# State space mixer: decay sums and sample inputs by broadcast DMA in place of TensorE products

## The chip, the cores and the metric

One Trainium2 chip, one core. The metric is the device time of one execution in microseconds. The engines are TensorE (PE in the rows), VectorE (DVE), ScalarE (ACT), GpSimd (POOL) and SyncE (SP), which only issues transfers here.

## What is computed

Two layers of a decoder over 512 prompt tokens and 8 sample tokens of width 1024: attention and gated linear attention, a squared ReLU layer, a state space mixer, and a second squared ReLU layer. The change lies in the state space mixer alone. Cut to what matters (8 groups of 4 heads, head width 64, state width 128, chunks of 128 tokens):

```python
xdt = x * dt[..., None]                                   # (chunk, token, group, head, 64)
cum = cumsum(dt * a_neg, axis=token)                      # within a chunk
seg = exp(where(causal, cum[t] - cum[s], -inf))
cb = einsum('tk,sk->ts', cm, bm)
y_intra = einsum('ts,jts,sjp->tjp', cb, seg, xdt)
to_end = exp(cum[last] - cum)
u = einsum('sk,sj,sjp->jpk', bm, to_end, xdt)             # into the state of the chunk
state = exp(cum[last]) * state + u
y_inter = einsum('tk,jpk,tj->tjp', cm, state, exp(cum))
```

A sample token is a chunk of length one with a state of its own: state = exp(dt a) state + dt x B, y = state C.

## The kernel before

Everything is in fp32. A fp32 product on TensorE stands in the rows as two MATMUL records (x2 for each product). Weights come in units of 128 x 1024 (512 KB) through a ring of 8 slots, loaded by SyncE as slots come free.

The mixer works group by group (`ssd_mix(g, d, project, products)` on TensorE, `mix(...)` on VectorE and ScalarE, `states(g)` on GpSimd), and each group carries along the six projections of the next one (`project(0)` to `project(5)`: two of x, then B, C, and two of the gate z). Group 0 stands by itself, groups 1 to 6 are three turns of a loop of two groups, and group 7 stands by itself: it has no next group, and products of the output projection (L1095) take the place of the six projections. Each engine runs its instructions in the order in which they are written and waits on semaphores; nearly every VectorE instruction is also waited for before the next (`mdo`, `cdo`).

TensorE's order in a group, with the lines of the profile:
1. `ssd_tokens`: transposes of B (L948) and of the samples (L950); sums of the decays in token order, over a chunk and over samples (L951 to L953); after ScalarE's roots of the group before, the transposes of x (L959).
2. `project(0)` (L517), `sample_outer(g, 0)` (L972): the outer products of the sample inputs with B into PSUM, from `sxdiag`, a diagonal spread that GpSimd makes (L468). Then `ssd_cb` (L979).
3. `project(1)`, `sample_outer(g, 1)`, `ssd_spread` of heads 2 and 3 (L994): a product that spreads the running decay sums of a head over all 128 partitions of a PSUM bank.
4. `project(2)`, `ssd_spread` of heads 0 and 1.
5. `project(3)` with `sample_y` (L1007) between its products, which reads the stepped states and waits for `ssm_stepped`; `ssd_intra` (L1023, L1028), which waits for `seg_ready`.
6. `project(4)`, `ssd_inter` (L1037), `project(5)`, `ssd_norm` (L1044).

ScalarE copies a finished projection into `xe` and `xs` (`conv_in`), makes the tanh of the convolution (`conv_tanh`), and the exponentials: `efeat` (L1384) from the spread sums in PSUM, and `seg` (L1385) from VectorE's differences. At the end of a group it takes the tanh of gate part 1, loads the table of the root (L1399) and takes the roots (L1401, L1403).

VectorE's order in a group: copies of the sums and of the samples (L1959, L1960); sxdt (L1962), xdt (L1967); the normalizing of the group before (L1936, L1938); `step_states(0)` (L1978), adding the outer products from PSUM to the decayed states; `prepare` and the taps of part 0 of the next group (L1882 to L1898); xde (L1993), the masked cb (`cbm`, L1996); `finish` of part 0, taps of part 1; `step_states(1)`; `differences` of heads 2 and 3 (L1983: spread sum less own sum, not above 0, from PSUM to `seg`); finish 1, taps 2; differences of heads 0 and 1; four products seg x cbm (L2013); finish 2, taps 3; the chunk states (L2029 to L2033), and the outputs.

GpSimd loads the states of a group (1 MB), makes `sxdiag`, multiplies the states by their decays in two halves (L477), and stores them.

Of the kernel before, what the change touches and what calls it, by code (L numbers as in the profile page):

```python
# [14 lines left out]
F32 = mybir.dt.float32  # L15
U32 = mybir.dt.uint32
ALU = mybir.AluOpType
# [3 lines left out]
P = 128  # L21
D = 1024
DC = D // P
TP = 512
NB = 8
# [74 lines left out]
PW = 120  # L100
LEAST = -3.0e38
# [40 lines left out]
def build(nc, A):  # L142
    ctx = ExitStack()
    with ctx:
# [118 lines left out]
        dts = sb("dts", [P, 8, NT + 1, CH_ALL], stack=c)  # L263
        dtg = sb("dtg", [P, 2, NT + 1, CJ], stack=c)
        dag = sb("dag", [P, 2, NT + 1, CJ], stack=c)
# [10 lines left out]
        cum = sb("cum", [P, 2, NT, CJ], stack=c)  # L276
        dec = sb("dec", [P, NT, CJ], stack=c)
        toend = sb("toend", [P, NT, CJ], stack=c)
# [13 lines left out]
        ssamp = sb("ssamp", [NB, 3, P], stack=c)  # L292
        sxdt = sb("sxdt", [NB, CJ, CHD], stack=c)
        sadg = sb("sadg", [NB, 2, NB, CJ], stack=c)
        sadec = sb("sadec", [P, NB, CJ], stack=c)

        sxdiag = seg[0:NB].rearrange("k j t q -> k (j t q)").rearrange("k (b c) -> k b c", b=NB)
# [4 lines left out]
        pssm = sb("pssm", [P, CJ, CHD], stack=c)  # L302
        c.close()

# [96 lines left out]
        def _(pool):  # L401
# [59 lines left out]
            def states(g):  # L461

                pool.dma_start(flat(ss0[:]), A["ssm0"][g]).then_inc(sem("ssm_in"), 16)

                if g:
                    pool.wait_ge(sem("y_intra"), g)
                pool.wait_ge(sem("sxdt_ready"), g + 1)
                nc.gpsimd.tensor_tensor(sxdiag, flat(sxdt[:]).unsqueeze(1).to_broadcast((NB, NB, GW)),  # L468
                                        deltac[:].unsqueeze(2).to_broadcast((NB, NB, GW)), ALU.mult).then_inc(
                    sem("sxdiag_ready"), 1)  # L470

                pool.wait_ge(sem("ssm_in"), g * 16 + 16)
                pool.wait_ge(sem("sadec_ready"), g + 1)
                for half in (slice(0, NB // 2), slice(NB // 2, NB)):
                    s = ss0[:, half].rearrange("p b j q -> p (b j) q")
                    decays = sadec[:, half].rearrange("p b j -> p (b j)").unsqueeze(2)
                    nc.gpsimd.tensor_tensor(s, s, decays.to_broadcast((P, NB // 2 * CJ, CHD)), ALU.mult).then_inc(  # L477
                        sem("ssm_decayed"), 1)
# [4 lines left out]
                pool.wait_ge(sem("ssm_out"), g * 16 + 16)  # L483
# [21 lines left out]
        def _(pe):  # L505
# [438 lines left out]
            def ssd_tokens(g, d):  # L944
# [4 lines left out]
                for i in range(3):  # L949
                    pe.transpose(B[7][0:NB, 32 + i * P:32 + (i + 1) * P], conv[:, d, i, TP:T], ident[:])  # L950
                mm(B[7][:, 0:16], tri[:], flat(dag[:, d, 0:NT]), start=True, stop=True)  # L951
                mm(B[7][:, 16:32], ones, flat(dag[:, d, 0:NT]), start=True, stop=True)
                mm(B[7][:, 416:448], ones[0:NB], flat(sadg[:, d]), start=True, stop=True).then_inc(  # L953
                    sem("ssd_turned"), 1)
# [7 lines left out]

            def sample_outer(g, half):

                if half == 0:
                    pe.wait_ge(sem("xdt_ready"), g + 1)
                    pe.wait_ge(sem("sxdiag_ready"), g + 1)
                else:
                    pe.wait_ge(sem("ssm_stepped"), g * 2 + 1)
                for j in range(2):  # L970
                    b = 4 * half + 2 * j
                    x = mm(B[4 + j][:], ssamp[:, 2, :], sxdiag[:, b:b + 2, :].rearrange("k b c -> k (b c)"), start=True, stop=True)  # L972
                x.then_inc(sem("ssm_outer"), 1)
# [9 lines left out]
            def ssd_spread(g, d, heads):  # L983

                for j in heads:
                    if j == 2:
                        pe.wait_ge(sem("cbm_ready"), g + 1)
                    if j == 3:
                        for read in ("small_read", "ssamp_read", "sadec_ready"):
                            pe.wait_ge(sem(read), g + 1)  # L990
                    if j == 0:
                        pe.wait_ge(sem("ssm_stepped"), g * 2 + 2)
                    for t in range(NT):
                        x = mm(B[4 + j][:, t * P:(t + 1) * P], dag[:, d, t, j:j + 1].to_broadcast((P, P)), tri[:],  # L994
                               start=True, stop=True)
                    x.then_inc(sem("decays_spread"), 1)

            def sample_y(g, d, products):


                pe.wait_ge(sem("decays_featured"), g * 4 + 1)
# [11 lines left out]
            def ssd_intra(g):  # L1013

                for j in (2, 3, 0, 1):
                    if j == 2:
                        pe.wait_ge(sem("seg_ready"), g * 4 + 2)
                    if j == 0:
                        pe.wait_ge(sem("seg_ready"), g * 4 + 4)
                        pe.wait_ge(sem("decays_featured"), g * 4 + 4)  # L1020
# [26 lines left out]
            def ssd_mix(g, d, project, products=2 * DC):  # L1047
# [5 lines left out]
                sample_outer(g, 0)  # L1053
                ssd_cb(g, d)
                project(1)
                sample_outer(g, 1)
                ssd_spread(g, d, (2, 3))
                project(2)
                ssd_spread(g, d, (0, 1))
# [17 lines left out]
            for j in range(1, SSD_UNITS):  # L1077
                ssd_project(0, j)
            ssd_mix(0, 0, lambda j, between=None: ssd_project(1, j, between))
# [54 lines left out]
        def _(act):  # L1134
# [195 lines left out]
            run(flat(dts[:, 2]), flat(dts[:, 1]), ACT.Exp).then_inc(sem("dt_expd"), 1)  # L1330
# [917 lines left out]
```

## Time and profile before

| | us |
|---|---|
| median of 3 runs | 1935.43 (1935.29 to 1935.89) |
| the profiled execution's own time | 1935.07 |
| its span, first to last instruction | 1933.3 |
| TensorE busy | 1856.6 |
| VectorE busy | 1065.1 |
| ScalarE busy | 354.3 |
| GpSimd busy | 147.2 |

The mean granted clock of TensorE was 0.96 of full speed (1.00 is 2.4 GHz, 0.50 is 1.2 GHz). Busy time is that of records; on TensorE the records of neighbouring products overlap, so that the chain's lengths are what a product costs. "idle before" in brackets is how long the engine had nothing, and what ended it. "issue" is time in which nothing that the profile shows was waited for.

### The profile page before, as it was taken

Reading aid. Unit: us, or ns where it says so; the run is one execution under the profiler, and the core shown is the slowest. Engines: PE = TensorE matmul, PEld = TensorE weight load, DVE = VectorE, ACT = ScalarE, POOL = GpSimd, SP = SyncE. Lnnn points to the kernel's source line nnn. Section 1 sums busy time; section 2 is a strip of 40 time slices with the busy share of each in tenths; the row PEclk is TensorE's granted clock in tenths of the full one; section 3 lists DMA queues with packets and bytes.
Section 4 is the critical chain, followed back from the end, with each engine's and each line's share of the span. In section 5 each row is a group of like instructions: output and inputs, shape, how many; then the busy total and the mean of one; then the engine's idle time right before and its main releaser. Section 6 shows DMA issues by size and latency. Waiting matters only on the chain.

```text
span 1933.3 us, 23888 instructions
## 1 busy us (share of the span) xinstructions
PE 1856.6 (96%) x8882; PEld 1562.0 (81%) x8882; DVE 1065.1 (55%) x2013; ACT 354.3 (18%) x856; POOL 147.2 (8%) x188
## 2 busy tenths in 40 slices
PE   7999989998999999989999999999999999999995
PEld 5776688776888888878888878888888888888884
DVE  4443753537544454555687778778643544445454
ACT  2322001111220032011222222322110121012100
POOL 0000220000000000000111011101100000000001
PEclk9999959788999999998999999999999999999997
DMA  7111531004545756541123212221303342343221
GB/s 248 58 55 56 174 120 44 24 17 164 223 176 217 267 192 238 195 154 54 49 97 102 91 44 101 95 82 57 112 34 130 110 153 92 146 169 149 88 87 44
DMA packets 47586, 227.43 MB, mean 118 GB/s; under 512 B 7080, under 2 KB 10168, under 8 KB 44416
## 3 DMA queue, kind: packets, MB, share of 16 engines
q1 hardware_dynamic: 37312, 123.74, 18.8%
q0 software_dynamic: 10032, 102.30, 13.8%
q8 instruction: 61, 1.00, 0.2%
q14 instruction: 37, 0.30, 0.1%
q10 hardware_dynamic: 144, 0.09, 0.0%
HBM read 210.78 MB, written 82.40 MB: 152 GB/s over the span
## 4 chain that ended last, share of the span: by engine, by line
PE 87%; DVE 7%; DMA 2%; ACT 2%; issue 2%; POOL 0%; DVEq 0%; SPq 0%; ACTq 0%
PE bank L904 40%; PE bank L517 30%; PE bank L1095 2%; PE bank L994 2%; PE bank L659 1%; PE bank L972 1%; PE bank L1023 1%; PE bank L619 1%; PE bank L603 1%; PE bank L1007 1%; DVE rstd L1435 1%; PE bank L1028 1%; DMA ring<-units 1%; DMA gath<-cache_v 1%; PE bank L1037 1%
## 5 line engine op out<-in xcount | busy, mean ns | idle before, releaser
L517 PE MATMUL bank<-hn,ring 128*128 128x260 f32 x2304 | 553.6, 393 | 5.5 <-DVE hn L1453 4.5
L517 PEld LDWEIGHTS bank<-hn,ring 128*128 128x128 f32 x2304 | 434.1, 194 | 77.0 <-issue 14.3
L904 PE MATMUL bank<-hid,ring 128*128 128x260 f32 x1024 | 231.0, 382 | 0.0
L904 PEld LDWEIGHTS bank<-hid,ring 128*128 128x128 f32 x1024 | 194.6, 190 | 29.9
L904 PE MATMUL bank<-hid,ssum 128*128 128x260 f32 x768 | 174.2, 382 | 0.0
L904 PEld LDWEIGHTS bank<-hid,ssum 128*128 128x128 f32 x768 | 145.9, 190 | 22.4
L904 PE MATMUL bank<-hn,ring 128*128 128x260 f32 x512 | 124.9, 387 | 2.8 <-DVE hnt L1712 2.8
L904 PE MATMUL bank<-hnt,ring 128*128 128x260 f32 x512 | 123.2, 383 | 0.0
L1732 DVE TENSOR_TENSOR u<-bank,p1c 128x260 f32<-128x260 f32 x48 | 20.6, 429 | 184.7 <-PE bank L904 183.1
L904 PE MATMUL bank<-hnt,ssum 128*128 128x260 f32 x512 | 118.9, 385 | 1.8 <-DVE hid L1741 1.8
L904 PEld LDWEIGHTS bank<-hn,ring 128*128 128x128 f32 x512 | 98.3, 192 | 18.6 <-DVE hnt L1712 3.2
L904 PEld LDWEIGHTS bank<-hnt,ssum 128*128 128x128 f32 x512 | 97.9, 191 | 17.5 <-DVE hid L1741 2.2
L904 PEld LDWEIGHTS bank<-hnt,ring 128*128 128x128 f32 x512 | 97.6, 191 | 15.1
L1737 DVE TENSOR_TENSOR u<-bank,u 128x260 f32<-128x260 f32 x48 | 20.6, 429 | 123.0 <-PE bank L904 122.8
L1296 ACT ACTIVATE hid<-hid 128x260 f32<-128x260 f32 x96 | 40.3, 420 | 258.0 <-DVE hid L1738 178.3
L517 PE MATMUL bank<-mixT,ring 128*128 128x260 f32 x224 | 65.7, 459 | 9.9 <-DVE h L1684 9.9
L1898 DVE SCALAR_TENSOR_TENSOR conv<-xe,pg,conv 128x512 f32<-128x512 f32 x96 | 72.2, 752 | 3.4
L1143 ACT ACTIVATE hn<-h 128x520 f32<-128x520 f32 x40 | 25.0, 635 | 262.9 <-DVE h L1768 153.4
L517 PEld LDWEIGHTS bank<-mixT,ring 128*128 128x128 f32 x224 | 50.8, 231 | 25.6 <-DVE h L1684 12.4
L1308 ACT ACTIVATE p1c<-bank 128x260 f32<-128x260 f32 x48 | 18.6, 387 | 244.9 <-PE bank L904 244.9
L904 PE MATMUL bank<-hn,ssum 128*128 128x260 f32 x256 | 61.3, 382 | 0.0
L517 PE MATMUL bank<-yout,ring 128*128 128x260 f32 x256 | 58.1, 391 | 2.4 <-DVE h L1684 2.4
(338 smaller groups left out, 2340.1 us busy)
## 6 DMA issues: line engine op xcount, KB each, us to landing
ring<-units SPq DMA_DIRECT2D x224, 512.0 KB, 4.1
ss<-ssm POOLq DMA_DIRECT2D x8, 1024.0 KB, 5.8
out_ssm<-ss POOLq DMA_DIRECT2D x8, 1024.0 KB, 5.8
out_win_k<-cache_k POOLq DMA_DIRECT2D x8, 1022.0 KB, 8.8
out_win_v<-cache_v POOLq DMA_DIRECT2D x8, 1022.0 KB, 6.4
gath<-cache_k POOLq DMA_DIRECT2D x24, 256.0 KB, 3.8
gath<-cache_v POOLq DMA_DIRECT2D x24, 256.0 KB, 3.7
h<-xT SPq DMA_DIRECT2D x4, 520.0 KB, 5.3
```

The costliest lines, as they stand in the source:

```text
L517: x = mm(half(n), ring[:, s, k], src[:, first + k, cols], start=start and k == blocks[0], stop=last and k == blocks[-1])
L603: mm(B[4 + j][:, 0:(j + 1) * P], qr[rows, j * P:(j + 1) * P], kr[rows, 0:(j + 1) * P], start=True, stop=True).then_inc(sem("scored"), 1)
L619: mm(B[7][AD * e:AD * e + AD, kt * P:TP], vtok[:, kt, AD * e:AD * e + AD], pt[:, PT_AT[kt]:PT_AT[kt] + TP - kt * P], start=kt == 0, stop=k ...
L659: x = mm(out[:, hp, b, :], gath[:, n % SLOTS, i, hp * P:(hp + 1) * P], spt[:, i, b * AH + 2 * hp:b * AH + 2 * hp + 2], start=b == 0 and hp ...
L904: x = mm(bank[:, 0:LO], weight(m, w, q % (DC // 2)), operand(m, q), start=q == 0 and m not in (2, 3), stop=q == every - 1, skip_group_chec ...
L994: x = mm(B[4 + j][:, t * P:(t + 1) * P], dag[:, d, t, j:j + 1].to_broadcast((P, P)), tri[:], start=True, stop=True)
L1095: x = mm(bank(n), ring[:, w, k], yout[:, part * DC + k, cols], start=part == 0 and k == 0, stop=part == 1 and k == DC - 3, skip_group_chec ...
L1143: run(hn[:, k], h[:, k], ACT.Square).then_inc(squares, 1)
L1296: ins = run(out, src, ACT.Relu)
L1732: do(V.tensor_tensor(u2[:], B[5][:, 0:LO], p1c[:], ALU.add), "banks_read")
L1737: do(V.tensor_tensor(u3[:], B[7][:, 0:LO], u2[:], ALU.add), "banks_read")
L1898: cdo(V.scalar_tensor_tensor(out, xe[:, j, tap:tap + TP], pg[:, d, 4 * j + tap:4 * j + tap + 1], out, ALU.mult, ALU.add), "taps_done" if t ...
```

## The change

For all eight groups at once, ahead of group 0, a table is made (`tab`, 100 columns per group): dt, the running sums, the decays of chunks, the decays to the chunk's end, and the sample decays. The running sums of all 32 heads also go as rows to a DRAM scratch (`cums`), from which GpSimd's queue broadcasts four heads per group over all partitions, straight into `seg` in SBUF. The dt-weighted sample inputs of a group go to a second scratch (`sxs`) and come back broadcast (`xb`). The outer products with B become eight `scalar_tensor_tensor` on VectorE, from SBUF. The differences are made in place in `seg`. All of `efeat` is made ahead of the first difference, since it reads what the differences overwrite.

GpSimd, per group:

```diff
-                pool.dma_start(flat(ss0[:]), A["ssm0"][g]).then_inc(sem("ssm_in"), 16)
                 if g:
                     pool.wait_ge(sem("y_intra"), g)
+                else:
+                    pool.wait_ge(sem("tab_begun"), 1)
+                    pool.dma_start(cums, cumrows).then_inc(sem("rows_out"), 16)
+                    pool.wait_ge(sem("rows_out"), 16)
+                pool.dma_start(flat(seg[:]), cums[CJ * g:CJ * g + CJ].rearrange("j t -> (j t)").unsqueeze(0)
+                               .to_broadcast((P, CJ * TP))).then_inc(sem("cums_in"), 16)
+                if g:
+                    pool.wait_ge(sem("ssm_out"), g * 16)
+                pool.dma_start(flat(ss0[:]), A["ssm0"][g]).then_inc(sem("ssm_in"), 16)
                 pool.wait_ge(sem("sxdt_ready"), g + 1)
-                nc.gpsimd.tensor_tensor(sxdiag, flat(sxdt[:]).unsqueeze(1).to_broadcast((NB, NB, GW)),
-                                        deltac[:].unsqueeze(2).to_broadcast((NB, NB, GW)), ALU.mult).then_inc(
-                    sem("sxdiag_ready"), 1)
+                pool.dma_start(sxs[g].rearrange("(b c) -> b c", b=NB), flat(sxdt[:])).then_inc(sem("rows_out"), 16)
+                pool.wait_ge(sem("rows_out"), g * 16 + 32)
+                if g:
+                    pool.wait_ge(sem("ssm_stepped"), g * 2)
+                pool.dma_start(flat(xb[:]), sxs[g].unsqueeze(0).to_broadcast((P, NB * GW))).then_inc(
+                    sem("sx_in"), 16)
                 pool.wait_ge(sem("ssm_in"), g * 16 + 16)
-                pool.wait_ge(sem("sadec_ready"), g + 1)
...
-                pool.wait_ge(sem("ssm_out"), g * 16 + 16)
```

TensorE: the calls of `sample_outer` and `ssd_spread` and both functions are gone; L951 to L953 and one of the three transposes of samples (L950) too. `sample_y` waits for `cbm_ready` in place of an efeat. Ahead of group 0:

```diff
+            pe.wait_ge(sem("dt_folded"), 2)
+            for t in range(NT):
+                x = mm(B[4][0:CH_ALL, t * P:(t + 1) * P], dts[:, 1, t], tri[:], start=True, stop=True)
+            x.then_inc(sem("cums_summed"), 1)
+            mm(B[6][:, 0:NT * CH_ALL], tri[:], flat(dts[:, 1, 0:NT]), start=True, stop=True)
+            mm(B[6][:, NT * CH_ALL:2 * NT * CH_ALL], ones, flat(dts[:, 1, 0:NT]), start=True, stop=True)
+            mm(B[6][:, 2 * NT * CH_ALL:512], ones[0:NB], flat(sad), start=True, stop=True).then_inc(
+                sem("cums_summed"), 1)
+            pe.wait_ge(sem("tab_ready"), 1)
```

ScalarE, in `mix` (and ahead of group 0 a copy of the sums to rows and three exponentials of the table):

```diff
-                act.wait_ge(sem("ssamp_read"), g + 1)
-                run(flat(sadec[:]), B[7][:, 416:448], ACT.Exp).then_inc(sem("sadec_ready"), 1)
                 run(flat(btok[:]), B[6][:], ACT.Copy).then_inc(sem("btok_ready"), 1)
-                act.wait_ge(sem("cum_left"), g + 1)
-                run(flat(dec[:]), flat(cum[:, 1]), ACT.Exp).then_inc(mstep, 1)
-                run(flat(toend[:]), flat(toend[:]), ACT.Exp).then_inc(sem("decay_exps"), 1)
...
+                act.wait_ge(sem("ssamp_read"), g + 1)
+                act.wait_ge(sem("cums_in"), g * 16 + 16)
+                for j in range(CJ):
+                    rows = slice(CHD * (j % 2), CHD * (j % 2) + CHD)
+                    run(efeat[rows, j // 2, :], flat(seg[:, j])[rows, P:TP], ACT.Exp).then_inc(
+                        sem("decays_featured"), 1)
                 for i, j in enumerate((2, 3, 0, 1)):
-                    act.wait_ge(sem("decays_read"), g * 4 + (i + 1))
-                    rows = slice(CHD * (j % 2), CHD * (j % 2) + CHD)
-                    run(efeat[rows, j // 2, :], B[4 + j][rows, P:TP], ACT.Exp).then_inc(sem("decays_featured"), 1)
+                    act.wait_ge(sem("seg_bounded"), g * 4 + (i + 1))
```

The new efeat stand behind the tanh of part 1 of the next group, ahead of this loop. VectorE, in `mix` (a copy of the group's table, `tabg`, takes the place of the copies and differences of the sums, and three copies of `prepare` are gone):

```diff
                 def step_states(half):
-                    dve.wait_ge(sem("ssm_outer"), g * 2 + (half + 1))
+                    if half == 0:
+                        dve.wait_ge(sem("sx_in"), g * 16 + 16)
                     dve.wait_ge(sem("ssm_decayed"), g * 2 + (half + 1))
-                    for j in range(2):
-                        b = 4 * half + 2 * j
-                        s = ss0[:, b:b + 2].rearrange("p b j q -> p (b j q)")
-                        mdo(V.tensor_tensor(s, s, B[4 + j][:], ALU.add), "ssm_stepped" if j else None)
+                    for b in range(4 * half, 4 * half + 4):
+                        s = flat(ss0[:, b])
+                        mdo(V.scalar_tensor_tensor(s, xb[:, b], conv[:, d, 2, TP + b:TP + b + 1], s, ALU.mult,
+                                                   ALU.add), "ssm_stepped" if b % 4 == 3 else None)
...
-                step_states(0)
...
+                def differences(j):
+                    for t in range(NT):
+                        own = F_CUM + CJ * t + j
+                        mdo(V.tensor_scalar(seg[:, j, t], seg[:, j, t], tabg[:, own:own + 1], 0.0, ALU.subtract,
+                                            ALU.min), "seg_bounded" if t == NT - 1 else None)
+
+                dve.wait_ge(sem("decays_featured"), g * 4 + 4)
+                differences(2)
+                differences(3)
+                step_states(0)
                 step_states(1)
-                for i, j in enumerate((2, 3)):
-                    dve.wait_ge(sem("decays_spread"), g * 4 + (i + 1))
-                    differences(j)
+                differences(0)
+                differences(1)
                 if nxt is not None:
                     finish(nxt, 1 - d, 1)
                     taps(nxt, 1 - d, 2)
-                for i, j in enumerate((0, 1)):
-                    dve.wait_ge(sem("decays_spread"), g * 4 + (i + 3))
-                    differences(j)
```

Ahead of group 0 VectorE copies dt and the running sums into the table and takes the sums to the chunk's end; the wait is `tab_ready`, for VectorE and TensorE both.

## Rows read from the trace of the kernel before

**Rows 1.** The page, part 1: busy time, share of the span and instructions.

```profile
PE 1856.6 (96%) x8882; PEld 1562.0 (81%) x8882; DVE 1065.1 (55%) x2013; ACT 354.3 (18%) x856; POOL 147.2 (8%) x188
```

**Rows 2.** The chain in order of time: start, length, engine, line.

```profile
924.00 1.02 PE bank L959 x8
...
1051.58 1.09 PE bank L959 x8
...
1061.59 1.09 PE bank L979 x8
...
1069.70 1.91 PE bank L972 x4
1071.61 1.98 PE bank L994 x16
...
1080.60 1.78 PE bank L994 x16
1082.39 0.44 PE bank L517 x2
...
1092.97 2.50 PE bank L1023 x32
...
1112.80 0.39 ACT gz L1360
...
1377.52 1.09 PE bank L959 x8
```

**Rows 3.** The timeline of TensorE: start, length, line, operation.

```profile
1115.40 1.09 PE L959 MATMUL bank<-ident,conv 128*128 128x128 f32 x8 [0.31 <-ACT ystd L1401]
...
1137.16 2.74 PE L994 MATMUL bank<-tri,dag 128*128 128x128 f32 x16 [1.73 <-DVE cbm L1996]
```

**Rows 4.** The timeline of VectorE.

```profile
1069.06 1.22 DVE L1993 TENSOR_TENSOR turns<-xdt,toend 128x1024 f32<-128x1024 f32 x1
...
1093.85 0.55 DVE L1895 TENSOR_SCALAR conv<-xe,pg 128x512 f32<-128x512 f32 x1 [0.41 <-ACT xs L1345]
1094.43 2.33 DVE L1898 SCALAR_TENSOR_TENSOR conv<-xe,pg,conv 128x512 f32<-128x512 f32 x3
...
1117.51 0.19 DVE L1959 COPY cum<-bank 128x32 f32<-128x32 f32 x1 [3.18 <-issue]
```

**Rows 5.** The timeline of GpSimd.

```profile
1052.88 3.59 POOL L468 TENSOR_TENSOR seg<-sxdt,deltac 8x2048 f32<-8x2048 f32 x1 [13.64 <-DVE sxdt L1962]
1056.45 4.21 POOL L477 TENSOR_TENSOR ss<-ss,sadec 128x1024 f32<-128x1024 f32 x2
```

**Rows 6.** The timeline of ScalarE.

```profile
1077.71 0.48 ACT L1384 ACTIVATE efeat<-bank 64x384 f32<-64x384 f32 x1 [2.36 <-DVE seg L1983]
1078.09 0.62 ACT L1385 ACTIVATE seg<-seg 128x512 f32<-128x512 f32 x1
```

**Rows 7.** Groups by line and shape, 880 to 1540, VectorE: busy, mean ns | idle.

```profile
L1898 DVE SCALAR_TENSOR_TENSOR conv<-xe,pg,conv 128x512 f32<-128x512 f32 x96 | 72.2, 752 | 3.4
L1983 DVE TENSOR_SCALAR seg<-bank,cum 128x128 f32<-128x128 f32 x128 | 44.9, 351 | 9.3 <-PE bank L994 3.6
L2013 DVE TENSOR_TENSOR seg<-seg,cbm 128x512 f32<-128x512 f32 x32 | 22.1, 692 | 1.1
...
L2031 DVE TENSOR_TENSOR std<-st,dec 128x256 f32<-128x256 f32 x24 | 10.2, 425 | 0.8
...
L1988 DVE TENSOR_SCALAR yT<-conv,pg 128x520 f32<-128x520 f32 x16 | 7.9, 491 | 0.6
```

**Rows 8.** TensorE in slices: length, busy (records), granted clock, DMA share, GB/s.

```profile
1138.00:1140.00 2.00, 2.00 (x12) 0.59 0.00 0
1140.00:1142.00 2.00, 2.00 (x6) 0.56 0.00 0
```

**Rows 9.** The page, part 6: DMA issues, KB each, median us to landing.

```profile
ss<-ssm POOLq DMA_DIRECT2D x8, 1024.0 KB, 5.8
...
out_pssm<-pssm POOLq DMA_DIRECT2D x8, 128.0 KB, 1.9
```

More of the change, by code:

```diff
@@ L100 @@
 PW = 120
+F_DT, F_CUM, F_DEC, F_END, F_SAMPLE = (CJ * i for i in (0, NT + 1, 2 * NT + 1, 3 * NT + 1, 4 * NT + 1))
+TAB = F_SAMPLE + CJ * NB
 LEAST = -3.0e38
@@ L948, in ssd_tokens @@
                     pe.transpose(B[6][:, t * P:(t + 1) * P], conv[:, d, 2, t * P:(t + 1) * P], ident[:])
[L949 to L954, printed above, removed]
+                for i in range(2):
+                    x = pe.transpose(B[7][0:NB, i * P:(i + 1) * P], conv[:, d, i, TP:T], ident[:])
+                x.then_inc(sem("ssd_turned"), 1)
                 for t in range(NT):
@@ L981, in ssd_cb @@
                 x.then_inc(sem("cb_ready"), 1)
[L983 to L996, printed above, removed]
             def sample_y(g, d, products):
-                pe.wait_ge(sem("decays_featured"), g * 4 + 1)
+                pe.wait_ge(sem("cbm_ready"), g + 1)
                 pe.wait_ge(sem("ssm_stepped"), g * 2 + 2)
@@ L1413, in _ @@
             gate(0, 0, 1)
+            act.wait_ge(sem("cums_summed"), 1)
+            run(cumrows, B[4][0:CH_ALL, :], ACT.Copy).then_inc(sem("tab_begun"), 1)
+            act.wait_ge(sem("cums_summed"), 2)
+            by_chunk = lambda first, count: B[6][:, first:first + count * CH_ALL].rearrange(
+                "p (t g j) -> p g t j", t=count, g=CG)
+            by_group = lambda first, count: tab[:, :, first:first + count * CJ].rearrange(
+                "p g (t j) -> p g t j", j=CJ)
+            run(by_group(F_DEC, NT), by_chunk(NT * CH_ALL, NT), ACT.Exp).then_inc(sem("tab_begun"), 1)
+            run(by_group(F_SAMPLE, NB), by_chunk(2 * NT * CH_ALL, NB), ACT.Exp).then_inc(sem("tab_begun"), 1)
+            act.wait_ge(sem("dt_folded"), 3)
+            run(by_group(F_END, NT), by_group(F_END, NT), ACT.Exp).then_inc(sem("tab_ready"), 1)
             mix(0, 0, 1)
@@ L1967, in mix @@
                     mdo(V.tensor_tensor(xdt[:, 2 * i:2 * i + 2], pair(4 + i),
-                                        dtg[:, d, 2 * i:2 * i + 2].unsqueeze(3).to_broadcast((P, 2, CJ, CHD)),
+                                        steps[:, 2 * i:2 * i + 2].unsqueeze(3).to_broadcast((P, 2, CJ, CHD)),
                                         ALU.mult), "xdt_ready" if i else None)
@@ L2030, in mix @@
                         continue
-                    mdo(V.tensor_tensor(std1[:], st[:, t - 1], dec[:, t].unsqueeze(2).to_broadcast((P, CJ, CHD)),
+                    mdo(V.tensor_tensor(std1[:], st[:, t - 1], decays[:, t].unsqueeze(2).to_broadcast((P, CJ, CHD)),
                                         ALU.mult))
@@ L2072, in _ @@
             gate(0, 0, 1)
+            by_group = lambda first, count: tab[:, :, first:first + count * CJ].rearrange(
+                "p g (t j) -> p g t j", j=CJ)
+            do(V.tensor_copy(by_group(F_DT, NT + 1), dts[:, 0].rearrange("p t (g j) -> p g t j", g=CG)))
+            dve.wait_ge(sem("tab_begun"), 3)
+            sums = lambda i: B[6][:, i * NT * CH_ALL:(i + 1) * NT * CH_ALL].rearrange(
+                "p (t g j) -> p g t j", t=NT, g=CG)
+            do(V.tensor_copy(by_group(F_CUM, NT), sums(0)))
+            do(V.tensor_tensor(by_group(F_END, NT), sums(1), by_group(F_CUM, NT), ALU.subtract), "dt_folded")
+            dve.wait_ge(sem("tab_ready"), 1)
             mix(0, 0, 1, None)
```

82 lines of the change are left out of this document (32 added, 50 removed).

## The prediction

> **What bounds the kernel now.** I read the page first, then the chain that ended last, then the timelines of single groups. On the page TensorE is busy for 96% of the span and VectorE for 55% [rows 1]; what matters is the stage of the eight groups, the only one that changes. The chain in order of time runs there through TensorE almost alone [rows 2]: the transposes of x of group 0 begin at 924.00, those of group 7 at 1377.52, so seven groups take 453.5 us. In the group that begins at 1051.58 the reader should see one product after another, with no pause in which a unit of weights waits. Only at the end of a group does the chain leave TensorE: projection 5 ends at 1112.80, ScalarE then gates, loads its table and takes roots, and the next transposes begin at 1115.40, after TensorE sat idle for 0.31 [rows 2, 3]. These 2.60 us are ScalarE's, and work taken from TensorE inside them brings nothing. Two groups are longer: VectorE begins them 3.18 us late, at the turn of its loop, and TensorE waits 1.73 us for its mask product [rows 3, 4].
>
> **A yardstick.** I call the start of the x transposes p0; an undisturbed group lasts 1115.40 - 1051.58 = 63.82. I walk through a changed group by the order of the code and the durations of the rows, and ask when the next p0 comes.
>
> **What leaves TensorE.** The outer products of the samples (L972) come twice per group, 1.91 each time (one stands), the spread decay sums (L994) take 1.98 and 1.78 [rows 2]: together 7.58 us per group. The small products L951 to L953 and one transpose (0.8 us) lie in the 2.60 us of ScalarE, so they are worth nothing except in group 0. Were TensorE alone the bound, eight groups would save 61 us.
>
> **What VectorE must now deliver.** TensorE starts projection 3, with the sample outputs between its products, only once all states are stepped. Before, it got there at 1082.39, that is p0 + 30.81 [rows 2]. Without the 7.58 it is there at p0 + 23.2: transposes 1.09, cb 1.09, and projections 0 to 2 at 7.01 each (L994 ends at 1071.61 + 1.98 = 1073.59, the next begins at 1080.60). When has VectorE stepped the states?
> - Taps of part 1 read what ScalarE copies out of projection 1. That ends at p0 + 16.2; from the end of a projection to the first tap 0.88 us pass (projection 3 ends at 1092.97, the tap on its copy begins at 1093.85) [rows 2, 4]. So p0 + 17.1. VectorE is there at about the same time: before, xde began at 1069.06 [rows 4], p0 + 17.5; without the first states (1.4 and a wait of 0.5) and three little copies of 0.3 each, and with xde, cbm and one finish (1.2 + 0.7 + 0.7) behind it, that is p0 + 17.3. GpSimd's decays end earlier now, since its 3.59 us of sample products are gone [rows 5], and VectorE's normalizing beside them is less disturbed, which gives VectorE perhaps 1 us back. I take 17.1.
> - The four taps take 0.58 + 2.36 = 2.94 [rows 4]: p0 + 20.0.
> - New wait. VectorE may not overwrite the sums before ScalarE has made all four efeat, and ScalarE makes them behind the tanh of part 1, which needs these taps. One efeat takes 0.48 and the next instruction starts 0.38 after it; the tanh and the exponential of 512 take about 0.6 [rows 6]. 0.55 + 3 x 0.4 + 0.55 = 2.3: p0 + 22.3. VectorE idles here, in every group, where it had none before.
> - Differences of heads 2 and 3. From PSUM 128 columns take 351 ns. A column costs 1.04 ns (256 more of them 692 - 425 = 267), so 218 of the 351 are fixed. From SBUF a tensor_scalar of 520 columns takes 491 in all, less than its columns alone would at that rate (542) [rows 7], so it goes at twice the rate and 128 columns should take 491 - 392 x 0.52 = 287. With 30 ns between them 8 take 2.54: p0 + 24.8.
> - The states. Eight scalar_tensor_tensor of 256 columns, all from SBUF, in place of four additions. 512 columns take 752; 256 fewer are worth 267 [rows 7]. 485 + 30 each, 4.1 in all: p0 + 29.0, where the transfers have landed.
>
> So TensorE, ready at 23.2, waits until 29.0: **5.8 us of the 7.58 come back as a wait.** Behind it the chain is as before: from 1082.39 to 1115.40, 33.01 us. VectorE has slack there (its differences of heads 0 and 1, a finish, a tap and four products end near p0 + 38.5, the projection near 39.6). The group lasts 29.0 + 33.0 = 62.0, 1.8 less than now.
>
> **The clock.** After the wait of 1.73 us the granted clock fell: the slices of 2 us behind it read 0.59 and 0.56, so about 3.4 us at 1.2 GHz in place of 2.4 [rows 8], and lost 1.7 us. A wait of 5.8 us is longer, and it comes in seven groups. I charge 1.7 us for each, and bound it from 0 (if the fall lay within the wait) to 3.4 (twice as long). The Trainium skill, "TensorE: Matmul & The Clock Gate", Part 1, says that idle time throttles the array to half and that the cost is half of the throttled time, and it shows a kernel that is throttled anew at each wait; the trace agrees in its one-wait case, and it is what speaks against this change.
>
> **The other kinds of group.** Group 0 has no earlier group to normalize, but its taps of part 1 hang on projection 1 as well, so it lasts the same. In the two groups at the loop's turn VectorE starts 2.4 later, of which 1.0 is covered by that projection: 1.4 more each. Group 7 has no next group: no taps, so the efeat are early, and VectorE has stepped by about p0 + 18 while TensorE arrives at 23.2. There the full 7.58 is gained. Sum of groups 0 to 6: 7 x (62.0 + 1.7) + 2 x 1.4 = 448.8 against 453.5, **4.7 less**.
>
> **The preparation.** Ahead of group 0, TensorE makes seven products (16 passes; 12 of 128 columns at 1.98/16 = 0.12 and 2 of 256 at twice that, 2.0 us), ScalarE two exponentials (0.35 and 0.4), VectorE a copy and a difference from PSUM (0.35 each), ScalarE one more (0.35): 4.0 us with the hand-overs, all serial behind the last projection, 0.8 given back by the small products gone from group 0: +3.2, and half a clock loss, 0.8 (this idle time is near 1.9 us). Between 2.5 and 6; I take 4.0. VectorE's other new work there (the tables' copy, the sample sums) lies beside projections.
>
> **DMA.** Per group two broadcasts of 1 MB and a row of 8 KB come to GpSimd's queue. Nearest rows: 1 MB of states lands in 5.8 us, 128 KB in 1.9 [rows 9]. The sums are sent at the end of the group before, some 33 us ahead of their use, and push the load of the states back by about 5 us, to about p0. The samples: row written by p0 + 2.4, broadcast landed by p0 + 8.3, decays (4.21 before [rows 5]) done by p0 + 7, all wanted at p0 + 24.8. Below, this costs nothing; above, it decides from 22 us for the samples' broadcast. I take nothing. In group 0 all four transfers follow each other, and the samples land near p0 + 15, still early.
>
> **Sum.** The profiled execution took 1935.07 (median of the runs 1935.43). 1935.07 - 4.7 - 7.6 + 4.0 = 1926.8; put to the median, **1927**.
>
> **Where a rule and a row part.** The nearest row of the same instruction is the 351 ns from PSUM. By it the eight differences would take 0.5 us more per group, and the sum would be 1931. The Trainium skill, "VectorE: DVE Perf Modes", section on mode 2x_2P, has tensor_scalar in fp32 from SBUF at two columns a cycle and gives no such mode to an instruction with two tensors, as the states' step now is. The 491 ns decide for 287.
>
> **Rivals.**
> - *The clock stays low for longer* (slower). At 3.4 us lost per wait: 7 x 1.7 = 11.9 more, **1939**, slower than now. The sign turns at 2.8 per wait. For it: the wait is three times as long as the one seen. Against: the fall also begins inside it, where it costs nothing. 0.19.
> - *No clock loss*: **1915**. Against it [rows 8]; for it, that the fall may end inside the wait. 0.09.
> - *VectorE is hidden, TensorE is the bound*: 61 less the 4 of the preparation: **1878**. It needs states stepped 5.8 us earlier than walked, and the taps hang on projection 1. 0.04.
> - *Broadcasts from one row are slow*: at 30 us in place of 5.8, 7 us per group late: **1980**. No row shows a broadcast. 0.05.
> - Forecast: 0.63.
>
> The range takes in the clock's price down to about 0 and up to 3.4 and half a microsecond per group in the walk: 1912 to 1942. What this kernel's measurement can tell from no change is about 0.2%, 3.9 us. Below 1931.5 lie most of the forecast and the two fast rivals: 0.59; within 0.2% the rest of the forecast and part of the first rival: 0.20; above it 0.21.
>
> **What would show it.** L972 and L994 gone; a wait of about 5.8 us of TensorE ahead of projection 3, ended by VectorE's step of the states, in groups 0 to 6 and not in 7; VectorE idle some 2.3 us for efeat; differences at 287 ns, steps at 485; granted clock of 0.5 for 3 to 4 us behind each wait; groups of 63.7. Wrong it would be if TensorE waited less than 4 us there or more than 7, if the releaser were a DMA, or if the low clock lasted past 5 us.

## The result and the profile after

The changed kernel took 1986.3 us (median of 4 runs, 1977.7 to 1999.5) against 1935.7 before: a ratio of 1.0263, 95% interval 1.0231 to 1.0295, slower by about 51 us. I had said 1927, with 1942 as the end of the range. The direction and the size are both wrong.

The profiled execution took 1987.23, its span 1985.4. The start of the x transposes, p0, divides the stage. Before, the groups 0 to 6 took 63.8 each, and 67.3 and 67.2 at the loop's turns. Now they take 76.1, 67.1, 67.6, 71.0, 74.8, 77.9 and 75.2: 509.7 in all against 453.6, so 56.1 more. From p0 of group 7 to the wait ahead of L1118 (now L1112) it is 62.95 against 70.74, so 7.8 less. p0 of group 0 comes at 927.45 in place of 923.92, 3.5 later. The sum is 51.8 of the 52.1 us by which the span grew; what lies outside this stage changed by 0.3. On the page, the line that answers to [rows 1] shows TensorE busy for only 4 us less, though products of some 61 us are gone: those that are left must have taken longer.

```profile
PE 1852.4 (93%) x8520; PEld 1567.1 (79%) x8520; DVE 1056.6 (53%) x2017; ACT 352.6 (18%) x836; POOL 128.7 (6%) x205
```

Group 2 on TensorE, the timeline: start, length, line, in brackets the idle time ahead and what ended it.

```profile
1070.65 1.09 PE L974 MATMUL bank<-ident,conv 128*128 128x128 f32 x8 [1.11 <-ACT ystd L1393]
1071.58 7.18 PE L535 MATMUL bank<-hn,ring 128*128 128x260 f32 x32
1078.60 1.05 PE L982 MATMUL bank<-conv 128*128 128x128 f32 x8
1079.49 14.19 PE L535 MATMUL bank<-hn,ring 128*128 128x260 f32 x64
1100.03 1.24 PE L535 MATMUL bank<-hn,ring 128*128 128x260 f32 x2 [6.35 <-DVE ss L1980]
1101.05 0.42 PE L995 MATMUL bank<-conv,ss 128*128 128x1 f32 x2
...
1115.76 2.57 PE L1011 MATMUL bank<-seg,xdt 128*64 128x128 f32 x32
```

This answers to [rows 2, 3]. L972 and L994 are gone, and in their place stands one wait of 6.35 us, ended by VectorE's last step of the states (29.4 us after p0). The 1.11 us ahead of L974 were 0.31 before; the small products are gone from a stretch that ScalarE bounds, and this is worth nothing, as said. What the reader should see next is the length of projection 3: from 1100.03 to 1115.76 it takes 15.7 us, where it took 10.6 [rows 2].

VectorE in the same group (timeline), then the two new kinds by shape (880 to 1540: busy, mean ns | idle), then ScalarE's four efeat.

```profile
1088.12 2.33 DVE L1898 SCALAR_TENSOR_TENSOR conv<-xe,pg,conv 128x512 f32<-128x512 f32 x3
1093.26 2.55 DVE L2000 TENSOR_SCALAR seg<-seg,tabg 128x128 f32<-128x128 f32 x8 [2.81 <-ACT efeat L1373]
1095.84 4.13 DVE L1980 SCALAR_TENSOR_TENSOR ss<-xb,conv,ss 128x256 f32<-128x256 f32 x8
```

```profile
L2000 DVE TENSOR_SCALAR seg<-seg,tabg 128x128 f32<-128x128 f32 x128 | 36.6, 286 | 23.8 <-ACT efeat L1373 19.5
...
L1980 DVE SCALAR_TENSOR_TENSOR ss<-xb,conv,ss 128x256 f32<-128x256 f32 x64 | 31.0, 485 | 2.8
```

```profile
1091.02 2.14 ACT L1373 ACTIVATE efeat<-seg 64x384 f32<-64x384 f32 x4
```

The walk holds step by step: 286 and 485 ns where 287 and 485 were worked out from [rows 7], and the new wait for efeat. The transfers are hidden. The two broadcasts land in 4.8 and 5.0 us, where the load of the states took 5.8 before; that load, behind a broadcast now, takes 7.5. GpSimd's timeline of group 2 and the page's DMA issues:

```profile
1071.19 0.51 POOL L484 DMA_DIRECT2D sxs<-sxdt  x1 [12.43 <-DVE sxdt L1964]
1073.49 0.53 POOL L488 DMA_DIRECT2D xb<-sxs  x1 [1.79 <-DMA sxs<-sxdt]
1074.04 3.77 POOL L496 TENSOR_TENSOR ss<-ss,tab 128x1024 f32<-128x1024 f32 x2
```

```profile
seg<-cums POOLq DMA_DIRECT2D x8, 1024.0 KB, 4.8
ss<-ssm POOLq DMA_DIRECT2D x8, 1024.0 KB, 7.5
xb<-sxs POOLq DMA_DIRECT2D x8, 1024.0 KB, 5.0
```

The samples' broadcast lands near 1078.5, 17 us before its first use. The granted clock of TensorE in group 2 (slices of 2 us: length, busy, granted clock, DMA share, GB/s):

```profile
1094.00:1096.00 2.00, 0.00 (x0) 1.00 0.59 174
1096.00:1098.00 2.00, 0.00 (x0) 0.63 0.23 88
...
1100.00:1102.00 2.00, 1.97 (x6) 0.50 0.00 0
...
1108.00:1110.00 2.00, 2.00 (x6) 0.50 0.03 8
1110.00:1112.00 2.00, 2.00 (x13) 0.95 0.00 0
```

The clock falls inside the wait and stays at 1.2 GHz for 10 us after it, through two thirds of projection 3. In group 4 the clock returns only at 1264, 25 us after the wait, behind projection 3 and the products of seg:

```profile
1238.00:1240.00 2.00, 1.35 (x5) 0.50 0.00 0
...
1260.00:1262.00 2.00, 2.00 (x18) 0.50 1.06 393
1262.00:1264.00 2.00, 2.00 (x18) 0.55 0.85 217
1264.00:1266.00 2.00, 2.00 (x11) 1.00 0.43 176
```

From such slices the time at 1.2 GHz can be added up: a slice of 2 us that reads c holds 4 x (1 - c) us of it, of which I count TensorE's busy share. At the low clock while working, the groups 0 to 6 spend 26, 9, 10, 11, 25, 26 and 26 us behind their waits, and group 7, which has no wait there, none. Group 4 is 74.8 us long; with 62.65 for a group without any fall (measured below) that is 12.1 more, half of its 25.

### The profile page after: what moved, and what is told of

The parts are those of the page before. It is cut to its first block, busy times and chain, and to the rows that moved or that the text cites. A ratio compares the mean times of both kernels' runs of the same rounds, so it can differ in the third digit from the quotient of the medians.

```text
span 1985.4 us, 23102 instructions
## 1 busy us (share of the span) xinstructions
PE 1852.4 (93%) x8520; PEld 1567.1 (79%) x8520; DVE 1056.6 (53%) x2017; ACT 352.6 (18%) x836; POOL 128.7 (6%) x205
## 4 chain that ended last, share of the span: by engine, by line
PE 81%; DVE 11%; issue 3%; ACT 2%; DMA 2%; DVEq 0%; POOL 0%; ACTq 0%; SPq 0%
PE bank L922 39%; PE bank L535 27%; PE bank L1089 2%; PE bank L677 2%; PE bank L1011 1%; DVE conv L1898 1%; PE bank L995 1%; DVE ss L1980 1%; DVE yrstd L1936 1%; PE bank L637 1%; PE bank L621 1%; PE bank L1016 1%; DVE rstd L1438 1%; DVE seg L2000 1%; DMA ring<-units 1%
## 5 line engine op out<-in xcount | busy, mean ns | idle before, releaser
L535 PE MATMUL bank<-hn,ring 128*128 128x260 f32 x2304 | 600.6, 415 | 55.6 <-DVE ss L1980 43.7
L535 PEld LDWEIGHTS bank<-hn,ring 128*128 128x128 f32 x2304 | 455.3, 205 | 129.8 <-DVE ss L1980 46.1
L922 PEld LDWEIGHTS bank<-hid,ssum 128*128 128x128 f32 x768 | 146.0, 190 | 22.3
L922 PE MATMUL bank<-hn,ring 128*128 128x260 f32 x512 | 124.8, 386 | 2.9 <-DVE hnt L1715 2.9
L922 PEld LDWEIGHTS bank<-hn,ring 128*128 128x128 f32 x512 | 98.3, 192 | 18.6 <-DVE hnt L1715 3.3
L995 PEld LDWEIGHTS bank<-conv,ss 128*128 128x128 f32 x256 | 71.9, 290 | 18.1
L922 PE MATMUL bank<-hn,ssum 128*128 128x260 f32 x256 | 61.3, 382 | 0.0
```

The lines of the kernel that those rows point to most:

```text
L535: x = mm(half(n), ring[:, s, k], src[:, first + k, cols], start=start and k == blocks[0], stop=last and k == blocks[-1])
L922: x = mm(bank[:, 0:LO], weight(m, w, q % (DC // 2)), operand(m, q), start=q == 0 and m not in (2, 3), stop=q == every - 1, skip_group_chec ...
L995: x = mm(B[6][:, n:n + 1], flat(ss0[:, b, 2 * i:2 * i + 2, :]), conv[:, d, 3, TP + b:TP + b + 1], start=True, stop=True, skip_group_check= ...
```

## The experiments

Theory A: all of the loss is TensorE's wait ahead of projection 3 and a low clock that outlives it. Rivals: the transfers or VectorE's new work slow TensorE by themselves (B). Within theory A, the clock stays low because of what TensorE works on when it comes back (A1), or because the wait is long (A2). The ratio is against runs of the kernel before on the same chip (its medians 1935.7 to 1936.6). The fourth column has the length of a group in which the clock never fell and which is no turn of the loop.

| kernel | us, median | ratio (95%) | group, undisturbed | low clock at work per group |
|---|---|---|---|---|
| changed | 1986.3 | 1.026 (1.023 to 1.030) | none | 9 to 26 |
| e1 states first | 1907.5 | 0.984 (0.980 to 0.988) | 57.6 | 0; 13 and 21 at the turns |
| e2 products apart | 1962.4 | 1.015 (1.012 to 1.018) | none | 12 to 13 |
| e3 fill | 1953.0 | 1.008 (1.005 to 1.010) | 62.65 | 0; 24 and 21 at the turns |
| e4 before, with a wait | 2052.2 | 1.060 (1.054 to 1.066) | none | 11 to 26 |
| e5 steps before taps | 1878.6 | 0.970 (0.968 to 0.972) | 56.0 | 0 |
| e6 efeat early | 1972.9 | 1.018 (1.016 to 1.020) | none | 3 to 25 |
| e7 states first, unrolled | 1882.8 | 0.972 (0.969 to 0.974) | 57.5 | 0 |
| e8 before, products apart | 1949.0 | 1.006 (1.004 to 1.007) | none | 3 to 13 |
| e9 e5, unrolled | 1872.8 | 0.967 (0.964 to 0.971) | 56.0 | 0 |
| e10 one product | 1912.8 | 0.988 (0.985 to 0.992) | none | 4 to 5 |

The last column leaves out the short fall of 1 to 3.4 us behind the preparation that some show in group 0.

**e4, the wait alone, in the kernel before.**

```diff
+                pe.wait_ge(sem("seg_ready"), g * 4 + 1)
                 project(3, sample_y(g, d, products))
```

> The kernel before, with one more wait on TensorE ahead of projection 3, for the first product of seg and cbm of the same group, which comes 5.8 us later than TensorE does. No broadcast, no new VectorE work. Theory A: the same fall of the clock and the same slow return, so about 5.8 + 9 us per group in seven groups and somewhat less in group 7: 2025 to 2050 us. Rival B (the slow return in the changed kernel comes of its broadcasts or its steps of the states): the clock returns after about 3.4 us as it did behind the wait of 1.7 us in the kernel before, so 5.8 + 1.7 per group: about 1990 us.

It took 2052, even above the range of theory A. The wait is 5.8 to 6.2 us in groups 0 to 6, nearly as long as in the changed kernel. Here is the timeline of TensorE and slices behind it, of group 1:

```profile
1040.77 1.23 PE L517 MATMUL bank<-hn,ring 128*128 128x260 f32 x2 [6.20 <-DVE seg L2014]
```

```profile
1042.00:1044.00 2.00, 2.00 (x9) 0.50 0.00 0
...
1062.00:1064.00 2.00, 2.00 (x16) 0.50 1.05 393
1064.00:1066.00 2.00, 2.00 (x22) 0.82 0.85 231
```

The fall is the same, and the return comes 24 us after the wait, as in the changed kernel's longer cases, without a broadcast and without a new VectorE instruction. The groups of 81 to 82 us are 63.8 + 5.8 + 12; groups 3 and 5 took 78 and 80. Rival B is out as the cause of the slow return.

**e3, work in place of the wait, in the changed kernel** (FILL is 14; nobody reads these products).

```diff
+                pe.wait_ge(sem("xdt_ready"), g + 1)
+                for k in range(FILL):
+                    mm(B[5][:, 0:LO], ones, hn[:, k % DC, 0:LO], start=True, stop=True)
                 project(3, sample_y(g, d, products))
```

> The changed kernel with 14 products of 260 columns (about 6.1 us) put ahead of projection 3 on TensorE, whose results nobody reads, so that it works through most of the time in which it waited. VectorE's and GpSimd's work and every transfer are the same. Theory A (the loss is the fall of the clock behind an idle array): the granted clock stays at 1.00 in groups 0 to 6 except perhaps at the loop's turn, projection 3 takes 10.6 us again, a group about 62.6, in all 1918 to 1930 us; group 7, which had no wait, is 6 us longer. Rival B (transfers or VectorE slow TensorE): projection 3 still takes 13 to 20 us, in all above 1975.

Groups 1, 2, 4 and 6 now take 62.65 to 62.8, with the clock at 1.00 throughout. They answer to the 62.0 of my walk, and to the changed kernel's own groups of 67 to 78 us, under the same transfers and the same VectorE work. The whole is 1953, not 1918 to 1930, because at the loop's turns a rest of the wait was left, and I had not given a rest of 3 us its price; without the excess of these two groups, 27 us, it would be 1926. Group 7, which had no wait to fill, is 6.1 us longer, as expected. TensorE and the slices in group 3:

```profile
1155.31 0.71 PE L536 MATMUL bank<-hn,ring 128*128 128x260 f32 x2 [2.90 <-DVE ss L1984]
```

```profile
1154.00:1156.00 2.00, 0.69 (x5) 1.00 0.00 0
1156.00:1158.00 2.00, 2.00 (x9) 0.50 0.00 0
...
1178.00:1180.00 2.00, 2.00 (x18) 0.52 0.90 248
1180.00:1182.00 2.00, 2.00 (x11) 1.00 0.36 145
```

2.9 us idle cost 24 us at the low clock; group 3 took 76.9. A2 is weakened here: this wait is shorter than half of the others and the fall lasts as long as the longest.

**e2, what follows the wait.**

```diff
-                project(3, sample_y(g, d, products))
+                outputs = sample_y(g, d, products)
+                project(3)
+                for m in range(products - 1):
+                    outputs(m)
```

> The changed kernel with projection 3 made in one piece and the 16 products of the sample outputs (128 x 1) in one block behind it, not between its products; TensorE's wait stays where it is. Theory A1 (the clock stays low behind the wait because projection 3 is mixed with one-column products): the clock is back within about 5 us of the end of the wait, before projection 3 is over, and of the 9 us that the clock costs per group some 6 or 7 come back: 1935 to 1950 us. Rival A2 (the length of the wait alone sets how long the clock stays low, 10 to 25 us): nothing changes beyond 1%, 1975 to 2000 us.

It took 1962, between the two, and the trace says why. TensorE in group 1, timeline and slices:

```profile
1025.40 9.93 PE L535 MATMUL bank<-hn,ring 128*128 128x260 f32 x32 [6.46 <-DVE ss L1983]
1035.16 4.59 PE L995 MATMUL bank<-conv,ss 128*128 128x1 f32 x32
1039.67 4.71 PE L1011 MATMUL bank<-seg,xdt 128*64 128x128 f32 x32
```

```profile
1028.00:1030.00 2.00, 2.00 (x6) 0.50 0.00 0
1030.00:1032.00 2.00, 2.00 (x9) 0.80 0.00 0
1032.00:1034.00 2.00, 2.00 (x11) 1.00 0.00 0
...
1038.00:1040.00 2.00, 2.00 (x11) 0.50 0.13 51
```

With plain products behind the same wait of 6.4 us the clock is back at about 1030.8, 5.4 us on. Then it falls a second time, at about 1037.6, in a stretch in which TensorE was never idle: during the block of 16 one-column products. All seven groups show both: the clock is back 5.3 to 6.1 us after the wait, waits of 9 us at the turns included, and falls again in the block. So A1 holds for the first fall, A2 does not, and the block pays for a fall of its own.

**e10, the price of the wait when nearly all one-column products are gone.** 15 of 16 products of the sample outputs are left out per group, so the samples' y is not computed.

```diff
                     for n in range(m * 2 * NB // (products - 1), (m + 1) * 2 * NB // (products - 1)):
+                        if n < 2 * NB - 1:
+                            continue
```

> The changed kernel with 15 of the 16 one-column products of the sample outputs left out in each group (the last one stays and signals), so that the samples' y is not computed; the wait of 6.4 us ahead of projection 3 and all else stays. It prices the return of the clock behind this wait when plain products follow. If the one-column products hold the clock low: 5 to 7 us at the low clock while TensorE works, some 3 us lost, groups of about 62.6 - 3.4 + 3 = 62, in all about 1915 us. If the length of the wait does it: 9 to 25 us of low clock as in the changed kernel, groups of 64 to 74, about 1960 us.

It took 1912.8, as A1 had it, with waits of 6.35 us as before. TensorE in group 2, timeline and slices:

```profile
1080.75 8.87 PE L535 MATMUL bank<-hn,ring 128*128 128x260 f32 x30 [6.35 <-DVE ss L1982]
```

```profile
1082.00:1084.00 2.00, 2.00 (x6) 0.50 0.00 0
1084.00:1086.00 2.00, 2.00 (x9) 0.78 0.00 0
1086.00:1088.00 2.00, 2.00 (x11) 1.00 0.00 0
```

The clock is back 3.8 to 4.7 us after each of the seven waits, TensorE works 4 to 5 us at the low clock, and the groups take 61.3. So behind plain products the low clock costs what I had charged or a little more, about 2.2 us. It is the one-column products between those of projection 3 that make 4.5 to 13 of it.

**e8, the block alone, in the kernel before** (the edit of e2, no wait added).

> The kernel before (no wait ahead of projection 3) with projection 3 in one piece and the 16 one-column products of the sample outputs in one block of about 4.6 us behind it. If a dense row of one-column products alone lets the clock fall, though TensorE is never idle, the granted clock reads 0.5 behind it in every group, for 3 to 10 us, and the kernel is slower by 1.0 (the block itself) plus 2 to 5 us per group: 1955 to 1985 us. If only idle time lets it fall, the clock stays at 1.00 and the kernel takes 1936 to 1945 us.

It took 1949, between the two expectations, as the low clock was short: 3.4 us in most groups. But it came in every group, in six of the eight without any wait of TensorE longer than 0.3 us. TensorE's timeline in group 1, where the block is followed by products of seg at the low clock:

```profile
1027.07 3.98 PE L1007 MATMUL bank<-conv,ss 128*128 128x1 f32 x32
1030.97 4.71 PE L1023 MATMUL bank<-seg,xdt 128*64 128x128 f32 x32
```

In groups 3 and 5, where a wait of 2 us stands ahead of L994, the low clock at work comes to 12 or 13 us, 6 behind the wait and 7 behind the block. Idle time is not needed for the clock to fall.

**e6, a shorter wait.** The four efeat move to the start of ScalarE's work on the group (behind btok).

> The changed kernel with the four efeat moved to the start of ScalarE's work on a group; nothing else. VectorE's idle time of 2.8 us ahead of the differences goes and TensorE's wait ahead of projection 3 shrinks from 6.4 to about 3.5 us. Theory A with a cost in proportion to the wait: the low clock shrinks too, from 9.6 to about 5 us lost per group, so the groups take 65 and the whole about 1935 us. Theory A with a slow return that hardly depends on the wait (once the clock is low, projection 3 with its one-column products holds it there): 2.8 us per group come back and little more, 1960 to 1975 us.

It took 1972.9, inside the second expectation. The wait is 3.6 us in place of 6.35 (6.3 in place of 9.1 at the turns), and the low clock at work is 24, 24, 3, 25, 10, 25 and 24 us. It is not in proportion to the wait. Groups 2, 4 and 6 have the same wait to a hundredth and the same products behind it, but the clock is back 4, 11 and 25 us after the wait, and they take 61.6, 64.9 and 71.4 us. The timeline of groups 2 and 6:

```profile
1102.48 1.10 PE L535 MATMUL bank<-hn,ring 128*128 128x260 f32 x2 [3.56 <-DVE ss L1980]
...
1378.21 0.71 PE L535 MATMUL bank<-hn,ring 128*128 128x260 f32 x2 [3.56 <-DVE ss L1980]
```

The same holds for repeated runs of the changed kernel: 1978 to 2000 us, where the kernel before, with far less low clock, stayed between 1929 and 1942 in all sets of runs. I can't say from the rows what decides how long it is.

**e1, the states first.** The theory's use: bring VectorE's answer forward.

```diff
+                step_states(0)
+                step_states(1)
                 dve.wait_ge(sem("decays_featured"), g * 4 + 4)
                 differences(2)
                 differences(3)
-                step_states(0)
-                step_states(1)
```

> The changed kernel with the step of the states moved ahead of the differences of heads 2 and 3, right behind the taps of part 1 (nothing else is changed). Theory A (the wait of TensorE ahead of projection 3 and the low clock behind it are the whole loss): VectorE ends the taps about 19.8 us after the start of the x transposes, the steps about 24.0, TensorE is there at 23.0, so the wait shrinks from 6.4 to about 1 us and the clock mostly stays up; a group takes about 57 us where it took 67 to 78, the two at the loop's turn some 60 to 65. In all about 1885 to 1900 us. Rival B (the new steps or the broadcasts slow something besides the wait, such as TensorE's reads): the groups stay above 62 us, in all over 1925.

It took 1907.5. The wait is 1.0 us in the groups within the loop's turns, and the clock stays up; they take 57.6, where 57 was expected. At the turns the wait is 3.8 and the low clock 13 and 21 us, so these two groups take 66.4 and 70.1, more than the 60 to 65 I gave them, and the whole is above my 1885 to 1900.

**e7, e1 with the loop of groups 1 to 6 written out.**

> e1_states_first with the loop of groups 1 to 6 written out on TensorE, ScalarE and VectorE (same instructions and waits, constants in place of registers). If VectorE's late start of 3.2 us at the loop's turn is the jump back, it goes: no wait of 3.8 us in groups 3 and 5, no fall of the clock there, all groups 57.6, in all about 1885 us. If it is the fetch of more code than is held, it stays or comes more often, up to every group: 1905 to 1960 us.

It took 1882.8, with all six groups at 57.5 to 57.8. VectorE's first copy of group 3, which had come 3.2 us late at the turn [rows 4], now follows at once (no idle time in brackets):

```profile
1098.80 0.42 DVE L1927 SCALAR_TENSOR_TENSOR gz<-gz,bank 128x260 f32<-128x260 f32 x1
1099.23 0.21 DVE L1957 COPY tabg<-tab 128x100 f32<-128x100 f32 x1
```

**e5, the states before the taps, efeat early, the products of seg before taps 2, the sample taps last.** Same instructions, same loop.

```diff
+                step_states(0)
+                step_states(1)
                 if nxt is not None:
                     finish(nxt, 1 - d, 0)
                     taps(nxt, 1 - d, 1)
...
                 dve.wait_ge(sem("decays_featured"), g * 4 + 4)
-                differences(2)
-                differences(3)
-                step_states(0)
-                step_states(1)
-                differences(0)
-                differences(1)
+                for j in (2, 3, 0, 1):
+                    differences(j)
...
-                    sample_taps(nxt, 1 - d)
```

> The changed kernel in another order, the same instructions: ScalarE makes the four efeat at the start of the group; VectorE steps the states behind cbm, ahead of finish 0 and the taps of part 1, then all differences, all products of seg and cbm, finish 1, the samples' outputs, taps 2 and 3, the chunk states, and only then the sample taps. By the walk VectorE has stepped the states at about 19.9 us after the start of the x transposes (22.3 at the loop's turn), ahead of TensorE's 23.0 in every group, and the products of seg stand when TensorE wants them. Theory A: no wait above 1.1 us, no fall of the clock in groups 1 to 6, groups of 56.5 to 57.5 us (up to 62 at the turn), in all 1872 to 1888 us. Rival: another wait takes its place (seg, chunk states) and brings the low clock again: above 1900 us.

It took 1878.6, within what theory A said. VectorE steps the states from 18.2 to 22.3 us after p0 (1042.05), ahead of TensorE:

```profile
1060.22 4.13 DVE L1980 SCALAR_TENSOR_TENSOR ss<-xb,conv,ss 128x256 f32<-128x256 f32 x8
```

TensorE doesn't wait for it. What is left are waits of 0.5 to 1.4 us ahead of the norm product, behind which the clock did not fall:

```profile
1040.04 1.14 PE L1032 MATMUL bank<-turns,normc 128*128 128x260 f32 x4 [0.63 <-DVE turns L2059]
```

**e9, e5 written out.**

> e5_steps_before_taps with the loop of groups 1 to 6 written out on TensorE, ScalarE and VectorE. The waits of 1.4 us ahead of the norm product in groups 2, 3 and 5, which follow VectorE's late start at the turns, should go: groups 1 to 6 all 56.0, 5.5 us less than e5_steps_before_taps, about 1873 us. If writing out costs instruction fetches elsewhere, no gain or a loss: 1878 to 1890.

It took 1872.8, 63.8 us or 3.3% below the kernel before. Groups 1 to 6 all take 56.04 us, 7.8 less than 63.8: the 7.58 us of removed products, and 0.2 that I have not placed.

## Why the prediction was wrong

1. **What leaves TensorE, 7.58 us per group.** Right: e9's groups are 7.8 shorter, and group 7, which has no wait, lost 7.8 in the changed kernel itself.
2. **The walk on VectorE.** Right in each term but one: taps end at 19.8 (20.0), differences 2.55 (2.54), states 4.13 (4.1), the end at 29.3 (29.0). The four efeat follow each other every 0.54 us, not 0.4, so their wait was 2.81 for 2.3. The wait of TensorE was 6.35 for 5.8, and a group with the clock held up takes 62.65 for 62.0. Over seven groups this is 4.5 us. At the turns the wait was 9.1, that is 2.7 longer where I had 1.4.
3. **The price of the clock.** This is the term that failed. I charged 1.7 us per wait, from one wait of 1.73 us [rows 8], with 3.4 as the upper bound, 7 x 1.7 = 12 in all. The groups lost 509.7 - 7 x 62.65 - 2 x 2.7 (the longer waits at the turns) = 66 us, 9.4 per group, from 4.5 to about 13. In the profiled executions the miss is 1987.2 - 1926.8 = 60.4: 54 of the clock (66 - 12), 4.5 and 2.6 of point 2, and less than 1 the other way from the rest. That the low clock would last past 5 us I had named as a sign of being wrong; it lasted 9 to 26 us of work. The row from which I priced was that of a wait ahead of L994 and a plain projection. The wait of the changed kernel stands ahead of projection 3, between whose products stand one-column products. Behind plain products the same long wait costs about 2.2 us (e10); behind these, 4.5 to 13 (changed kernel), and once as little as 1.7 (e6, group 2, behind 3.6 us). I had bounded the cost by the length of the fall that I had seen, and not asked what TensorE would be doing while it came back. My slower rival had the place and the sign, but 3.4 as its price.
4. **What the low clock costs.** By the Trainium skill, "TensorE: Matmul & The Clock Gate", Part 1, half of the throttled time is lost. The trace agrees, with 12.1 of 25 us in group 4. I had read there that only idle time throttles; this the runs do not bear out, for in e8 the granted clock read 0.50 for 3.4 us in groups in which TensorE waited nowhere longer than 0.3 us.
5. **The preparation**: p0 of group 0 is 3.5 us later, for 3.2 + 0.8. Right.
6. **The transfers cost nothing.** Right: 4.8 and 5.0 us to landing, 17 us ahead of use.
7. **VectorE's rate from SBUF.** Right: the differences took 286 ns, for 351 from PSUM. The Trainium skill, "VectorE: DVE Perf Modes", section on mode 2x_2P, gives fp32 tensor_scalar from SBUF two columns a cycle, and the trace agrees.

So the saving was real in TensorE's work, and was given back first as a wait behind VectorE (6.35 of 7.58), and then more than the rest of it was lost through the clock. Which waits were new was foreseen; how to price them was not.

To point 3 belongs a warning that the trace of the kernel before held outside the stage, and that I passed over. In the attention of the samples TensorE makes products of two columns (L659) from 249.9 to 292.8, with two waits of 0.3 and 1.5 us in between. The granted clock read 0.50 from 250.9 to 298.7, and came back 3.2 us after projections of 260 columns had begun again at 295.46. The timeline, and a slice of 10 us within it:

```profile
259.74 26.26 PE L659 MATMUL bank<-spt,gath 128*128 128x2 f32 x120 [0.30 <-DMA gath<-cache_v]
```

```profile
260.00:270.00 10.00, 10.00 (x48) 0.50 0.54 157
```

So 3.4 us was no bound for a fall where narrow products stand. That a few of them between wide ones make such a place, only the experiments show.

What stays open is how long the low clock lasts in a given group: behind the same wait and ahead of the same products it was 3, 10 or 24 us of work (e6). That behind one-column products the cost can be several times 1.7 us is shown; what decides its size in one group is not.

## What to carry to other kernels

Price a new wait on TensorE by what follows it, not by its length alone. Where one-column products stand between the wide ones, 3 us idle cost 10 to 12 us through the clock here (e3), besides the wait itself; ahead of plain products, 6 us idle cost 2 to 3 (e10, e2). When work moves from a saturated TensorE to VectorE, find first where in VectorE's order the results are wanted; the same instructions in another order turned 1986 into 1879 us. And a cost read from one case in a trace holds for the work that stood behind that case.

## What the runs showed of the hardware

- The granted clock of TensorE can fall with no wait of TensorE ahead of it: 16 one-column products in a row (32 records in 4.0 us) brought 1.2 GHz for 3.4 us and more, in all eight groups of e8 and in seven of e2; group 7 of e2 has the block too, in 3.6 us, and kept its clock. The same products, each between wide ones and at 2.4 GHz, never did so by themselves (the kernel before, e5, e9).
- Once the clock was at 1.2 GHz, that very mixture mostly kept it there: it returned 9 to 26 us after the wait, in two cases after 4 and 6 (changed kernel, e1, e3, e4, e6). With plain products it returned after 3.8 to 6.1 us, in 14 groups of 14 (e2, e10).
- A run of 192 records of two-column products (L659, the kernel before) went at 1.2 GHz nearly throughout: 47.8 us at that clock, with TensorE busy for 46 of them.
- Waits of 0.5 to 1.4 us ahead of projection 3 or of the norm product brought no fall in any group; those of 1.7 to 2.1 us ahead of L994, and all of 2.8 us and more ahead of projection 3, did. Length alone does not decide: the waits of 1.66 and 2.36 us behind the last group are in every run, and a fall of 3.4 us follows in the kernel before, e3, e7, e8 and e9, and none in the changed kernel and the others.
- VectorE's late start at the loop's turn, 3.2 us before and 3.6 in the changed kernel, goes when the loop is written out (e7, e9).
- A broadcast of one row of 8 KB from DRAM to 128 partitions (1 MB) lands no later than 1 MB of distinct data: 4.8 to 5.0 us against 5.8 [rows 9].
